# Branch B's keys and values as seven half-size products, through HBM, in a hybrid encoder layer

## The reference, cut to what matters

```python
h = layer_norm(x, ln_in_g, ln_in_b)                  # (512, 2048)
proj = h @ w_in[l]                                   # aq ak av ag | bq bk bv bf bg | cq cg | mg
oa = swa_sink_attention(aq, ak, av, sinks, rel_table)   # branch A, window 128
logf = log_sigmoid(bf + b_forget); cum_logf = cumsum(logf)
ob = forgetting_attention(bq, bk, bv, cum_logf)      # branch B, 16 heads of 64, causal
oc = memory_attention(cq, mk, mv)                    # branch C, 4 heads of 256, 256 memory tokens
branches = (oa * silu(ag), ob * silu(bg), oc * silu(cg))
merged = sum(sigmoid(mg_n + b_gate_n) * (branches[n] @ w_branch[n]) for n in range(3))
h = layer_norm(alpha * h + merged @ w_out[l], ln_g, ln_b)
```

## Time and profile before

| | us |
|---|---|
| median of 3 runs (1880.71 to 1882.14) | 1882.04 |
| profiled execution, device time | 1880.85 |
| its span, first to last instruction | 1879.3 |
| PE busy | 1850.4 (98%) |
| DVE busy | 1220.2 (65%) |
| ACT busy | 829.5 (44%) |
| mean granted TensorE clock | 0.996 |

### The profile page before, as it was taken

The page is one execution under the profiler, slowest core; times in us unless marked ns, Lnnn a source line. Parts: engine busy times, 40 slices in busy tenths (PEclk is TensorE's granted clock), DMA queues, the critical chain, the costliest instruction groups (busy, mean ns, idle before and its releaser), DMA issues.

```text
span 1879.3 us, 24337 instructions
## 1 busy us (share of the span) xinstructions
PE 1850.4 (98%) x8599; PEld 1527.8 (81%) x8599; DVE 1220.2 (65%) x1909; ACT 829.5 (44%) x1360; POOL 162.4 (9%) x225
## 2 busy tenths in 40 slices
PE   8999999999999999999999999999999999999996
PEld 6888887888888888888888888888888888888884
DVE  5854335645555545578789878878787645576776
ACT  4652222444444444344445545455456333234543
POOL 1100000000000000000000000000001000003223
PEclk9999999999999999999999999999999999999998
DMA  8654456433333333333342533615427544439988
GB/s 296 198 152 126 125 145 201 116 87 103 91 91 97 83 99 82 99 104 108 87 157 84 211 113 112 224 38 187 165 105 260 199 146 148 150 117 239 244 209 193
DMA packets 227033, 271.95 MB, mean 145 GB/s; under 512 B 12768, under 2 KB 150032, under 8 KB 224784
## 3 DMA queue, kind: packets, MB, share of 16 engines
q1 hardware_dynamic: 196400, 188.24, 32.1%
q0 software_dynamic: 30416, 82.22, 16.4%
q10 hardware_dynamic: 144, 0.52, 0.1%
HBM read 229.38 MB, written 37.32 MB: 142 GB/s over the span
## 4 chain that ended last, share of the span: by engine, by line
PE 95%; DMA 2%; DVE 1%; POOL 1%; ACT 0%; issue 0%; DVEq 0%; POOLq 0%; SPq 0%; ACTq 0%
PE acc L635 13%; PE acc L637 13%; PE acc L636 13%; PE scores L955 4%; PE scores L959 4%; PE scores L957 4%; PE transposed L662 3%; PE scores L1029 2%; PE acc L955 2%; PE scores L1030 2%; PE scores L1031 2%; PE acc L957 2%; PE acc L959 2%; PE acc L1029 2%; PE acc L1030 2%; PE acc L1031 2%
## 5 line engine op out<-in xcount | busy, mean ns | idle before, releaser
L635 PE MATMUL acc<-h_hi,w_lo 128*128 128x512 f32 x1056 | 420.6, 398 | 0.0
L637 PE MATMUL acc<-h_hi,w_hi 128*128 128x512 f32 x1056 | 412.0, 390 | 0.0
L636 PE MATMUL acc<-h_lo,w_hi 128*128 128x512 f32 x1056 | 411.1, 389 | 0.0
L1568 DVE TENSOR_TENSOR w_lo<-raw_weights,w_hi 128x1024 fp32r<-128x1024 f32 x214 | 260.9, 1222 | 229.9 <-ACT w_hi L1111 224.3
L1111 ACT ACTIVATE w_hi<-raw_weights 128x1024 fp32r<-128x1024 f32 x214 | 225.8, 1058 | 278.4 <-PE acc L637 115.7
L1359 ACT ACTIVATE piece_split<-w 128x512 fp32r<-128x512 f32 x336 | 211.9, 632 | 214.6 <-PE scores L959 78.4
L2013 DVE TENSOR_TENSOR piece_split<-w,piece_split 128x512 fp32r<-128x512 f32 x336 | 231.5, 691 | 81.5 <-ACT piece_split L1359 72.6
L637 PEld LDWEIGHTS acc<-h_hi,w_hi 128*128 128x128 f32 x1056 | 198.2, 188 | 42.5
L635 PEld LDWEIGHTS acc<-h_hi,w_lo 128*128 128x128 f32 x1056 | 198.9, 188 | 41.0 <-issue 2.8
L636 PEld LDWEIGHTS acc<-h_lo,w_hi 128*128 128x128 f32 x1056 | 198.6, 188 | 39.6 <-issue 1.0
L955 PE MATMUL scores<-piece_split,h_lo 128*128 128x512 f32 x288 | 112.3, 390 | 0.0
(11 more groups left out here) (413 smaller groups left out, 3403.1 us busy)
## 6 DMA issues: line engine op xcount, KB each, us to landing
raw_weights<-in_w_in SPq DMA_DIRECT2D x134, 512.0 KB, 3.8
w<-in_w_in SPq DMA_DIRECT2D x96, 512.0 KB, 7.4
raw_weights<-in_w_branch SPq DMA_DIRECT2D x48, 512.0 KB, 5.1
raw_weights<-in_w_mem_kv SPq DMA_DIRECT2D x32, 512.0 KB, 5.2
gate<-gate_scratch POOLq DMA_DIRECT2D x12, 1024.0 KB, 6.6
gate_scratch<-first_product POOLq DMA_DIRECT2D x12, 512.0 KB, 6.6
out_w_x<-in_w_out POOLq DMA_DIRECT2D x12, 512.0 KB, 7.7
x_rows<-in_x SPq DMA_DIRECT2D x4, 1024.0 KB, 8.7
```

The costliest lines, as they stand in the source:

```text
L635: pe.matmul(bank_out, wl, hi[:, k, :], start=first, stop=False)
L636: pe.matmul(bank_out, wh, lo[:, k, :], start=False, stop=False)
L637: return pe.matmul(bank_out, wh, hi[:, k, :], start=False, stop=last)
L1568: dve.tensor_tensor(w_lo[:, slot, :], raw[:, slot, :], w_hi[:, slot, :].bitcast(F32), ALU.subtract).then_inc(lo_ready, 1)
```

## The change: what it does

1. B's keys and values are two groups of seven half-size products, between C and B, with the code of the merge gates (`gate_group(g)` for g of 0 and 1). Their output (token rows) is stored to `kv_dram` in HBM.
2. A pass of B has 4 chunks: two for the queries of the next pair, two for the gate of this one. The keys of the next pair are loaded as rows and transposed by PE in this pass (`b_turn_k`, in place of `b_turn_v`); the values are loaded into the place of their low part (`load_v`) and split there. The hooks of the old chunks 4 to 7 are those of the new chunks 0 to 3. A's keys take the place of "the next queries" in the last pass.
3. The sums of h are made in the passes 0 to 2 of C (`sum_tiles`, at the steps of `SUMS_AT`), split there, and stored to HBM (`s_dram`); they are loaded for the groups. The passes of A don't make them.
4. S3 overwrites a quarter of h for a group; that quarter is kept in `a21_dram` and loaded back before B.
5. The forget logits come ahead of C. The Toeplitz stores move from B to C, two a pass. C's loop is written out on ACT and DVE.

```diff
+SUMS_AT = {(0, 3): 0, (0, 5): 1, (1, 1): 2, (1, 3): 3, (1, 5): 4, (2, 1): 5, (2, 3): 6, (2, 5): 7}
...
 # PE
+                hooks = {0: {5: lambda: b_scores_stage(0)},
+                         1: {7: lambda: (b_turn_stage(0, (0, 1)), b_scores_stage(1))},
+                         2: {0: lambda: b_turn_stage(0, (2, 3)), 7: lambda: b_values_stage(0)},
+                         3: {2: lambda: b_turn_stage(1, (0, 1)), 4: lambda: b_turn_stage(1, (2, 3)),
+                             7: lambda: b_values_stage(1)}}
+                if not last_pair:
+                    hooks[2][1] = lambda: b_turn_k(2 + i)
...
 # ACT, a pass of B
+                    if s == 1:
+                        act.wait_ge(v_loaded, 32 + 32 * i)
+                        act.activation(b_v[:, :, :, 0, :], b_v_raw[:, :, :, 1, :], ACT.Copy).then_inc(b_v_hi, 1)
                         b_exps(0)
+                    if s == 2:
                         b_probs_hi(0, (0, 1, 2, 3))
+                        if not last_pair:
+                            k_hi(2 + i)
                         b_exps(1)
+                        if not last_pair:
+                            q_hi(CH_P + 1, 4, i, acc[JOB_P % 2])
+                    split_hi(CH_P + s, 4, i)
...
 # ACT, a pass of C (before its split_hi)
+                    if (i, s - 1) in SUMS_AT:
+                        sums_hi(SUMS_AT[i, s - 1])
...
 # DVE, a pass of C
                     split_lo(CH_C + s, 8, i)
+                    if (i, s - 1) in SUMS_AT:
+                        sum_tiles_lo(SUMS_AT[i, s - 1])
                     if s < TT:
                         residual(s)
...
+                    if (i, s) in SUMS_AT:
+                        sum_tiles(SUMS_AT[i, s])
...
 # DVE, a pass of B
+                    if s == 1:
+                        dve.wait_ge(b_v_hi, 1 + i)
+                        dve.tensor_tensor(b_v[:, :, :, 1, :], b_v_raw[:, :, :, 1, :],
+                                          b_v[:, :, :, 0, :].bitcast(F32), ALU.subtract).then_inc(v_ready, 1)
+                        b_max(0)
                     if s == 2:
                         b_probs_lo(0, (0, 1))
                         b_max(1)
                         b_probs_lo(0, (2, 3))
+                        if not last_pair:
+                            k_lo(2 + i)
+                    split_lo(CH_P + s, 4, i)
+                    if s == 1:
                         b_normalise(0)
+                    if s == 2:
                         b_normalise(1)
+                            q_lo(2 + i, acc[JOB_P % 2], acc_free[JOB_P % 2])
...
 # POOL
+            for i in range(PAIRS):
+                if i:
+                    pool.wait_ge(gated, BT + i)
+                    pool.dma_start(br_dram[1, i - 1], b_sum[:, :]).then_inc(br_stored, 16)
+                    pool.wait_ge(b_o, 2 * i)
+                    load_v(i)
+                if i < PAIRS - 1:
+                    pool.wait_ge(k_turned, i + 1)
+                    load_k(i + 1)
```

More of the change, by code:

```diff
@@ L519, in _ @@
                     load_x((7, 9, 12, 15).index(n))
+            for s in range(2):
+                load(CH_F + s, (CH_F + s) % RING, tile(w_in[0], s, BF), CK)
             with sp.Fori(0, HC) as i:
@@ L801, in b_scores_stage, with b_turn_k, b_pass @@
+            for g in range(KV_GROUPS):
+                gate_group(g)
+            def b_turn_k(count):
+                pe.wait_ge(k_loaded, 16 * count)
+                for t in range(TT):
+                    last = pe.transpose(ob[:, t * P:(t + 1) * P], b_kr[:, t, :], ident[:, :])
+                last.then_inc(k_turned, 1)
+            def b_pass(i, last_pair=False):
                 def b_scores_stage(hh):
@@ new lines, in k_hi @@
+            def k_hi(count):
+                act.wait_ge(k_turned, count)
+                for hh in range(2):
+                    half = slice(hh * 64, hh * 64 + 64)
+                    act.activation(b_k1[half, hh, :], ob[half, :], ACT.Copy).then_inc(b_k_hi, 1)
+            for s in range(2):
+                split_hi(CH_B + s)
+            q_hi(CH_B + 1, 0, 0, acc[JOB_B % 2])
+            k_hi(1)
+            for done in (st_c11, st_c12, st_c21, st_c22):
+                act.wait_ge(done, 16 * KV_GROUPS)
@@ L1762, in _, with q_lo @@
-            steps.mark(dve.tensor_copy(f_parts[:, 2, :], f_n[:, :]))
-            steps.settle()
-            dve.sem_inc(f_ready, 1)
-            steps.close()
-            dve.wait_ge(br_stored, 16 * HC)
-            dve.wait_ge(r_stored, 16 * HC)
-            with dve.Fori(0, PAIRS) as i:
-                steps = Steps(dve, dve_b, 3, i)
+            steps.close()
+            def q_lo(count, bank, free):
+                dve.wait_ge(b_q_hi, 4 * count)
+                for hh in range(2):
+                    half, other = slice(hh * 64, hh * 64 + 64), slice(64 - hh * 64, P - hh * 64)
+                    last = dve.scalar_tensor_tensor(out=b_q2[other, hh, :], in0=bank[half, :], scalar=0.125,
+                                                    in1=b_q1[half, hh, :].bitcast(F32), op0=ALU.mult,
+                                                    op1=ALU.subtract)
+                last.then_inc(q_ready, 1)
+                dve.wait_ge(q_ready, 2 * HC + count)
+                dve.sem_inc(free, 1)
@@ new lines, in k_lo @@
+            def k_lo(count):
+                dve.wait_ge(b_k_hi, 2 * count)
+                for hh in range(2):
+                    half, other = slice(hh * 64, hh * 64 + 64), slice(64 - hh * 64, P - hh * 64)
+                    dve.tensor_tensor(b_k2[half, hh, :], ob[half, :], b_k1[half, hh, :].bitcast(F32), ALU.subtract)
+                    last = dve.tensor_copy(b_k2[other, hh, :], b_k1[half, hh, :].bitcast(F32))
+                last.then_inc(k_ready, 1)
+            for s in range(2):
+                split_lo(CH_B + s)
@@ L2108, in _ @@
+            for g in range(KV_GROUPS, GROUPS):
+                gate_group(g)
             for n in range(LOOKAHEAD):
@@ L2490, in load_branch @@
+            for v in range(2):
+                load_sum(S2_TILE, S2, v)
+            pool.wait_ge(multiplied, CH_B)
+            pool.wait_ge(r_stored, 16 * HC + 32)
+            load_s3()
+            for v in range(2):
+                load_sum(S4_TILE, S4, v)
             def load_branch(n, dst):
```

1205 lines of the change are left out of this document (625 added, 580 removed).

## The result

| | before | after |
|---|---|---|
| median | 1881.4 us (4 runs) | 2022.5 us (4 runs, 2019.4 to 2024.2) |
| ratio, 95% interval | | 1.075 (1.0731 to 1.0768) |
| profiled execution, device time | 1880.85 | 2019.4 |
| its span | 1879.3 | 2017.8 |
| mean granted TensorE clock | 0.996 | 0.968 |

What follows compares the result with a forecast made beforehand. PE, busy 98% of the span, was taken to bound the kernel. Against 1880.85 us, - 21.8 + 22 + 27 + 24.6 + 4.8 + 1.6 = + 58.2 gave 1939 us, range 1905 to 1962.

Steps and rivals of the forecast that it cites:

- 96 matmuls fewer: Keys and values of B take 672 matmuls instead of 768, at 0.227 us each: 21.8 us saved on PE.
- B, head 0: PE waits 3.0 to 3.2 us before head 0's transposes, behind the values' load, in 7 passes: 22 us.
- B, head 1: PE waits 2.1 us before head 1's transposes and 1.7 more for low probabilities, in 7 passes: 27 us.
- C: Passes 1 and 2: PE waits 11.5 us before the probabilities' transposes and 0.8 at the values, twice 12.3: 24.6 us.
- the clock: Two waits of 11.5 us in C may each slow PE's following matmuls, 2.4 us each: 4.8 us.
- ends of the groups: Between the last group and pass 0 of C, DVE is later than PE: 1.6 us; sum loads taken as hidden.
- so I take 34: C, passes 1 and 2: sum-tile stores issued at 27 to 28 us, behind Toeplitz and residual stores, taken as landed at 34.
- Pass 0 ... zero: C, pass 0: tiles too, but early rows and DVE done at 34.4 of 36.2 us, so no wait.
- The Trainium skill's rule on how many engines a transfer gets: C: two outermost rows mean two engines; tile stores share their rings and wait, giving 24.6 us rather than 18.
- third rival: The clock falls in B as well, 2.4 us more in each of 7 passes: 1956 us; chance 12%.
- first rival: The other engines keep up, B's and C's waits vanish and only PE's matmuls count: 1859 us; chance 10%.

Runs made afterwards that it cites:

- e9: e8's kernel with the LayerNorm rows of the next pass of C loaded early, ahead of the tiles' stores on POOL: 1865.4 us, ratio to before 0.9921.
- e11: As e1, Toeplitz copies from rows in HBM, but with the two heads outermost again instead of the 128 query rows: 1970.1 us.
- e1: Changed kernel with Toeplitz rows stored to HBM once, then copied from there with the 128 query rows outermost, two pairs a pass of C: 1968.7 us.
- e3: Changed kernel with the values' split moved behind head 0's exponentials and the chunk's split on ACT, behind head 0's normalisation on DVE: 1972.3 us.
- e4: Changed kernel with ACT's query copies behind the chunk's split and DVE's low queries behind head 1's low probabilities: 1995.6 us.
- e7: Changed kernel with the edits of e1, e3 and e4 together: 1894.8 us, ratio to before 1.008.
- e6: Changed kernel with B's values loaded ahead of the store of the last pair on POOL: 1974.3 us.
- e8: e7's kernel with the sum tiles moved behind the scores in C as well: 1892.8 us, ratio to before 1.0061.

## Why the prediction was wrong

The direction was right, and so were most of the places; two that it put at nothing, pass 0 of C and the entry of the groups, were not. Of the 79 us between its sum and the measured one, C makes 42 and the clock 22. Its terms, in us, against the profile:

| term | predicted | measured |
|---|---|---|
| 96 matmuls fewer | -21.8 | -21.8 by count; PE busy 1829.4 in e9 against 1850.4, -21.0 |
| B, head 0 | 22 | 34.2 (7 waits of 4.9) |
| B, head 1 | 27 | 22.3 (13.3 + 9.0) |
| C | 24.6 | 66.6 (12.9, 26.0, 24.9, and 2.8 for `c_q`) |
| the clock | 4.8 | 26.4 |
| ends of the groups | 1.6 | 9.5 (7.7 + 1.8) |
| sum | +58.2 | +137.2, of 138.5 |

**C is the term that failed.** The prediction had the mechanism: "The next tile must wait until the last is stored", behind two Toeplitz stores on the same queue. Then it wrote "so I take 34" for a store issued at 27 to 28. The store of pass 1 was issued 27.7 us after the pass began and landed after 49.8. The price stood in the rows and was not used: two Toeplitz stores of 17.3 one behind the other, issued at 6 and 7, end at 41, not at 34 with the tile's store behind them. Measured, the second of them landed at 44.8, 37.6 after its issue: two together move 27 GB/s where one alone moved 24 (the windows under e11), so a pair takes nearly twice as long as one. e1 puts the tile store's landing back to 5.4 us, and the waits are then 9.5 and 9.0 against the 11.5 predicted with that landing. So the DVE and ACT steps of this term were sound, a little too dear; only the landing was mis-sized. "Pass 0 ... zero" failed for the same cause in another place: I looked only for the tiles' wait, while a weight load on the other queue landed after 26.9 us. e1 took that wait away with the same edit.

The Trainium skill's rule on how many engines a transfer gets ("DMA: Bandwidth & Descriptors", "Why a DMA increments its semaphore by 16 and not by 1") was weighed there. The trace agrees on the number of engines (shares of 0.12 and 0.25), but e11 shows that this number alone cost nothing that PE felt: with two engines and another source the kernel is as fast as e1. What made the landing late was the source.

**The clock was the second.** With the same 8503 matmuls PE is busy 1855.8 in the changed kernel and 1829.4 in e9: 26.4 us. Only two of C's waits had been counted; there were three, one more at the entry of the groups (6.2), and seven in B, 13.6 by e3. The third rival had this, with 7 x 2.4 = 16.8, and its place was right; it was given 12% because the prediction asked whether *every* wait slows PE. The rows show that it is neither all nor none: in the changed kernel the clock was 0.53 behind head 0's 4.9 and 1.00 behind head 1's 1.9, and in e1, with the same code in B, 0.56 and 0.58 behind that 1.9 as well. The e3 and e4 edits took 24.5 of busy time from e1 (1860.2 to e7's 1835.7), 13.6 and 0.7 from the changed kernel; what e1 had more of it behind head 1 was paid back in shorter waits and cost no time. Head 0's wait was put at 3.1 and measured 4.9. No run has a wait of 3 in B, so what one of that size does to the clock stays open.

**B, head 0.** All links held but one. (As written they add up to a wait of 2.9, 15.4 less 12.5, not to the 3.0 to 3.2 stated.) The store was issued 3.5 us into the pass (3.4 predicted), the second load at 4.9 (4.8), PE wanted the transposes at 12.7 (12.5). The values landed 4.9 after the issue, not the 2.9 taken from the Toeplitz reads the earlier trace rows: at 9.8 for 7.7. e6 shows that 2.7 was to be had, with nothing ahead of it. **Head 1** was right: 1.90 for 2.1, 1.15 for 1.7; e4 shows that both go when the query copies and the low queries are moved. (13.15 less 11.2 is 2.0, where the text has 2.1.)

**The ends.** The 1.6 between the groups and pass 0 measured 1.8. The entry into the groups was put at nothing, or up to 6 if loads were not hidden: there a load of a group's weights took 13.4 us and PE waited 6.2. With the wide copies 2.0 are left.

The first rival needed all these waits to vanish and gave 1859. e9, which removes them by edits, is at 1865. In spans it is 16.8 under before: 21.0 of busy time, less the 1.9 and 1.8 that PE still waits at the entries of the groups and of B. The matmuls' saving was there all along, and was lost to the source of one transfer and to the order of three lists, those of ACT, DVE and POOL.

Left open: a store out of many partitions with two outermost rows was not tried, so that how the rate goes with the number of source partitions is known at one point. The old narrow stores were never left in B with the rest of the change, so what moving them to C cost by itself is not known. Nor were the rows loaded early without the moved sum tiles, which alone gained 0.4 us of span from e7 to e8: the 29.2 of e9 may be the rows' or need both. Which engines a transfer used is not in the trace, only how many were busy.

## What to carry to other kernels

Before moving a DMA, divide its KB by its landing time. 320 KB in 17.3 us beside 1024 KB in 8.0 says that it is slow, and a window with little else in flight (a share of 0.12) that it holds few engines. What is issued behind it can then wait as long, whoever issued it, as two tile stores and one weight load did here; price the waiter by that row, not by its own. A table that is read many times out of a few partitions was better stored to HBM once and copied from there (51.5 and 50.8 us less in e1 and e11). Where loads, stores and their waits share an issuer, ask for each one moved what now stands behind its wait. And when an edit creates waits, price each twice: its length, and the slow matmuls behind it (1.9 us behind each wait of 4.9 here, nothing in time behind those of 1.9), for each place and pass.

## What the runs showed of the hardware

- What a wait costs in clock does not follow from its length. Matmuls were 0.43 apart for 4.5 us behind a wait of 12.9, 5.4 behind 26.0, 2.8 behind 24.9 and 4.2 behind 4.9; behind the same 1.9 not at all in the changed kernel, and for some 4 us in e1. The Trainium skill, "TensorE: Matmul & The Clock Gate", Part 1, says that idleness takes the clock to half and activity gives it back; the trace agrees, and PE paid anew at each place and pass. I could not have foretold from the rows of before which of the short waits would pay.
- Stores whose source is two partitions moved 24 to 27 GB/s together, one or two at a time; the same copies out of HBM, two at a time, 76 GB/s on as many engines.
- A few busy DMA engines slow loads that another issuer made: a weight load of SP, 512 KB, landed after 26.9 us with the Toeplitz stores of POOL in flight (the median of such loads is 3.8).
- The high and low parts of a sum tile, the same size and issued 0.8 us apart, show landings of 4.9 and 22.1. Both count on one semaphore, so I read the first row as the moment when 16 of the 32 counts had come from either store, and trust only the last of such a pair. The Toeplitz stores, two on one semaphore as well, bear this out: the first of pass 0 shows 6.1 us, in which 27 GB/s move half of its 320 KB. No run gave the two stores semaphores of their own.
